# The scan of a diffusion-backbone layer: the turned inverse by whole-array transpositions instead of products of its own

## What is computed

```python
def rwkv7_scan(inputs, s0):
    def step(s, inp):
        r_t, w_t, k_t, v_t, kk_t, a_t = inp
        sa = jnp.einsum('bhvk,bhk->bhv', s, -kk_t)
        s = (s * w_t[:, :, None, :] + sa[..., None] * (kk_t * a_t)[:, :, None, :]
             + v_t[..., None] * k_t[:, :, None, :])
        return s, jnp.einsum('bhvk,bhk->bhv', s, r_t)
    xs = tuple(jnp.moveaxis(z.astype(jnp.float32), 1, 0) for z in inputs)
    s_last, y = lax.scan(step, s0, xs)
    return jnp.moveaxis(y, 0, 1), s_last
```

## Time and the profile before

| | |
|---|---|
| median of 3 runs | 4198.44 us |
| the three runs | 4198.46, 4190.90, 4198.44 us |
| span of the profiled execution | 4190.6 us |
| granted clock, mean | 0.939 |
| stage of the scan | about 1126 to 2395 us |

### The profile page before, as it was taken

How to read it: one execution, slowest core, us unless ns; L and a number is a source line. 1 busy time by engine, 2 the same in 40 slices (tenths; PEclk the granted TensorE clock), 3 DMA queues, 4 the chain that set the end, 5 groups by cost and what they waited for, 6 DMA issues and landing times. The chain is left out here.

```text
span 4190.6 us, 114323 instructions
## 1 busy us (share of the span) xinstructions
PE 3609.0 (86%) x50045; PEld 3216.5 (77%) x50045; DVE 2427.7 (58%) x4367; ACT 1876.2 (45%) x3279; POOL 1273.3 (30%) x1258
## 2 busy tenths in 40 slices
PE   5699999999777777777777678799399999999997
PEld 2578888888677777777777678777299999999987
DVE  3236676630047666767676765433567676666666
ACT  3246665631145554555454544233244344434454
POOL 1223333321056464556554245300101111010202
PEclk8899999999889999999999889899599999999999
DMA  5235555532333333333332267443366667676786
GB/s 171 68 120 177 188 175 170 170 130 72 112 76 92 84 84 80 86 100 86 84 93 66 63 194 224 138 141 115 102 197 206 206 206 216 194 216 200 230 288 226
DMA packets 565269, 612.66 MB, mean 146 GB/s; under 512 B 66018, under 2 KB 469284, under 8 KB 563748
## 3 DMA queue, kind: packets, MB, share of 16 engines
q1 hardware_dynamic: 515620, 493.82, 38.1%
q0 software_dynamic: 22688, 80.75, 6.5%
q10 hardware_dynamic: 26464, 30.77, 2.4%
HBM read 443.62 MB, written 161.50 MB: 144 GB/s over the span
## 5 line engine op out<-in xcount | busy, mean ns | idle before, releaser
L578 PE MATMUL moe_h<-moe_xt_hi,moe_w_hi 128*128 128x256 f32 x2048 | 582.6, 284 | 7.3 <-DVE moe_w_lo L430 3.4
L430 DVE TENSOR_TENSOR moe_w_lo<-moe_w_lo_whole,moe_w_hi 128x2048 fp32r<-128x2048 f32 x254 | 446.3, 1757 | 242.3 <-ACT moe_w_hi L646 195.5
L578 PE MATMUL moe_h<-moe_xt_lo,moe_w_hi 128*128 128x256 f32 x2048 | 580.3, 283 | 0.0
L578 PE MATMUL moe_h<-moe_xt_hi,moe_w_lo 128*128 128x256 f32 x2048 | 580.2, 283 | 0.0
L1963 PE MATMUL inward_pp<-u_u_hi,inward_w_hi 128*128 128x512 f32 (+1 forms) x1360 | 527.6, 388 | 20.6 <-POOL inward_w_lo L2123 20.6
L1963 PE MATMUL inward_pp<-u_u_lo,inward_w_hi 128*128 128x512 f32 (+1 forms) x1360 | 516.0, 379 | 0.0
L1963 PE MATMUL inward_pp<-u_u_hi,inward_w_lo 128*128 128x512 f32 (+1 forms) x1360 | 515.6, 379 | 0.0
L578 PEld LDWEIGHTS moe_h<-moe_xt_hi,moe_w_hi 128*128 128x128 f32 x2048 | 393.4, 192 | 18.3 <-issue 5.8
L578 PEld LDWEIGHTS moe_h<-moe_xt_lo,moe_w_hi 128*128 128x128 f32 x2048 | 393.5, 192 | 3.6
L578 PEld LDWEIGHTS moe_h<-moe_xt_hi,moe_w_lo 128*128 128x128 f32 x2048 | 393.4, 192 | 0.0
L486 POOL DMA_INDIRECT scratch_x<-moe_ys,moe_who x30 | 86.1, 2869 | 863.7 <-DVE moe_ys L752 746.7
(11 more groups left out here) (397 smaller groups left out, 9893.0 us busy)
## 6 DMA issues: line engine op xcount, KB each, us to landing
moe_w_lo_whole<-in_moe_w SPq DMA_DIRECT2D x384, 512.0 KB, 5.1
scratch_ops<-inward_ops SPq DMA_DIRECT2D x72, 514.0 KB, 3.8
scan_over<-scratch_ops SPq DMA_DIRECT2D x72, 512.0 KB, 10.1
inward_w_lo_whole<-in_w_in SPq DMA_DIRECT2D x38, 512.0 KB, 4.5
scan_aq<-scratch_ops SPq DMA_DIRECT2D x36, 516.0 KB, 5.3
scratch_gates<-inward_out SPq DMA_DIRECT2D x64, 256.0 KB, 2.1
all_late<-in_w_mod POOLq DMA_DIRECT2D x32, 512.0 KB, 4.4
rest_modsum<-scratch_gates SPq DMA_DIRECT2D x64, 256.0 KB, 3.4
```

Of the source, the lines that this page charges most:

```text
L430: return nc.vector.tensor_tensor(x_lo, x, x_hi.bitcast(F32), ALU.subtract)
L578: mm = nc.tensor.matmul(hb[ft % 2][m][:, 0:CAP], w_, x_, start=(k == 0 and part == 0), stop=(k == KD - 1 and part == 2))
```

## The change

T and Lt are gone: no product Lt, no mask and no unit addition for T, no T product and no T add in the levels. Instead, at each level `forward` lets PE turn the whole W (four transpositions of 128x128 per unit) behind the F products, into the same pair of PSUM banks, and ACT copies F and the turned W together, 1024 columns, into the new tile FT. A transposition of 128x128 turns two neighbouring blocks and both heads at once, which puts odd and even blocks on different halves of the partitions. F is therefore written by the parity of the block, and F's 16 products and W's 16 products each go over all four quadrants in turn. DVE adds the new part of W through a view of the tile with the parities apart. V moves to r=0 beside L, tK to r=3 beside tB, where V was; r=4 has no product of the solve any more. The waits for the over tiles move from the joint products to r=0.

```diff
@@ -2294,7 +2294,8 @@
         V, La, Lb, Lk = (twice(x) for x in ("V", "La", "Lb", "Lk"))
         over = each("over", [P, 2, 4 * G])
         ob = each("ob", [P, 2, G])
-        W, T, F, L = (each(x, [P, 2, G]) for x in "WTFL")
+        W, L = (each(x, [P, 2, G]) for x in "WL")
+        FT = each("FT", [P, 2, 2 * G])
         aq = each("aq", [P, 2, 2, 2 * G + 4])
...
@@ -2302,7 +2303,8 @@
         Sd = each("Sd", [P, 2, HD])
         X, Z = (each(x, [P, 2, HD]) for x in "XZ")
         y = each("y", [P, 8, HD])
-        bank = [[n.ps(f"b{u}{b}", [P, 512]) for b in range(4)] for u in U]
+        pair = [n.ps(f"pair{u}", [P, 2, 512]) for u in U]
+        bank = [[n.ps(f"b{u}{b}", [P, 512]) for b in range(2)] + [pair[u][:, x, :] for x in range(2)] for u in U]
         masks = n.sb("masks", [P, len(MASKS) * P])
         late, stack = env["late"], env["stack"]
         wm = late[:, 0:NJ * G].rearrange("p (k c) -> p k c", k=NJ)
...
-        level_pe = [x for m in LEVELS for x in (f"F{m}", f"W{m}", f"T{m}")][:-1]
+        level_pe = [x for m in LEVELS for x in (f"F{m}", f"T{m - 1}", f"W{m}")]
         chunks = lambda names: [f"{x}{c}" for c in range(4) for x in names]
 
         def steps(name, names):
@@ -2331,11 +2333,10 @@
         second_done = [EVICTED[FIRST_OF[u][1]][1] + "1" for u in U]
 
-        PE = [Steps(n.sem(f"pe_solve{u}"), ["L", "Lt"] + list(FIRST_OF[u]) + ["tB", "V", "tK"] + level_pe) for u in U]
-        AC = steps("act_solve", ["L", "tB", "V", "tK"] + [f"F{m}" for m in LEVELS])
-        DV = [Steps(n.sem(f"dve_solve{u}"), ["T0"] + [f"{x}{d}" for p in FIRST_OF[u] for x in EVICTED[p] for d in U] +
-                    [f"{x}{m}" for m in LEVELS for x in "TW" if m < 5 or x == "W"]) for u in U]
-        PO = steps("pool_solve", ["T0", "W0"] + [f"H{m}" for m in LEVELS])
+        PE = [Steps(n.sem(f"pe_solve{u}"), ["L", "V"] + list(FIRST_OF[u]) + ["tB", "tK"] + level_pe) for u in U]
+        AC = steps("act_solve", ["L", "V", "tB", "tK"] + [f"F{m}" for m in LEVELS])
+        DV = [Steps(n.sem(f"dve_solve{u}"), [f"{x}{d}" for p in FIRST_OF[u] for x in EVICTED[p] for d in U] + [f"W{m}" for m in LEVELS]) for u in U]
+        PO = steps("pool_solve", ["W0"] + [f"H{m}" for m in LEVELS])
@@ -2361,15 +2362,15 @@
         def four(x):
             return x.rearrange("p d (c f) -> p d c f", f=HD)
 
-        def banked(x):
-            return x[:, :].rearrange("p (d c f) -> p d c f", d=2, f=HD)
+        def halves_of(x):
+            return x[:, :, :].rearrange("p d (q j f) -> p j (d q) f", j=2, f=HD)
+
+        def products(u, half):
+            return pair[u][:, :, half * G:(half + 1) * G]
 
         def masked(name):
             k = MASKS.index(name)
             return masks[:, k * P:(k + 1) * P].rearrange("p (d f) -> p d f", d=2).unsqueeze(2).broadcast_to([P, 2, 4, HD])
-
-        def level_banks(m):
-            return (3, 2) if m % 2 else (2, 3)
 
         def lru_of(k):
             j, q = k // (2 * NG), k % (2 * NG)
@@ -2473,12 +2474,9 @@
                 uB, uK = (0, 1) if r == 1 else (1, 0)
                 for u in U:
                     if r == 1:
-                        AC[u].wait(pe, "L", it)
-                        DV[u].wait(pe, "T0", it)
+                        AC[u].wait(pe, "V", it)
                     else:
                         DV[u].wait(pe, EVICTED[FIRST_OF[u][0]][1] + "1", it)
-                pe.wait_ge(s_over0[uK], 16 * it + 16)
-                pe.wait_ge(s_over1[uK], 16 * it + 16)
                 for k in range(8):
                     mmB = side_by_side(uB, k, of_ops(ob[uB], None, 0), aq[uB][:, b], 0, False)
                     mmK = side_by_side(uK, k, of_ops(over[uK], None, G), over[uK], 2 * G, True)
@@ -2492,16 +2490,13 @@
                 if r == 0:
                     pe.wait_ge(s_aq[u][b], half * 16 + 16)
                     pe.wait_ge(s_ob[u], 16 * it + 16)
+                    pe.wait_ge(s_over0[u], 16 * it + 16)
+                    pe.wait_ge(s_over1[u], 16 * it + 16)
                     DV[u].wait(pe, "W5", it - 1)
-                    two(u, ("L", 2, oA, oB), ("Lt", 3, oA, oB))
+                    two(u, ("L", 2, oA, oB), ("V", 3, xV, unit))
                 elif r == 3:
                     DV[u].wait(pe, second_done[u], it)
-                    two(u, ("tB", 2, oB, unit), ("V", 3, xV, unit))
-                else:
-                    AC[u].wait(pe, "tB", it)
-                    for k in range(8):
-                        mm = one(u, 2, xK, unit, True, k)
-                    PE[u].did("tK", mm)
+                    two(u, ("tB", 2, oB, unit), ("tK", 3, xK, unit))
 
             def forward(u, m, a):
                 it = a[0]
@@ -2510,26 +2505,30 @@
                     DV[u].wait(pe, f"W{m - 1}", it)
                 else:
                     PO[u].wait(pe, "W0", it)
-                    AC[u].wait(pe, "V", it)
-                for k in range(8):
-                    mm = one(u, level_banks(m)[0], of(H[u][(m - 1) % 3]), of(W[u]), True, k)
+                    AC[u].wait(pe, "tK", it)
+                held, old = of(H[u][(m - 1) % 3]), of(W[u])
+                for pos in range(4):
+                    for j in range(2):
+                        k = 2 * pos + j
+                        for x, h in enumerate(HALVES):
+                            mm = nc.tensor.matmul(pair[u][HALVES[j], x, pos * HD:(pos + 1) * HD], held(h, k), old(h, k), start=True, stop=True)
                 PE[u].did(f"F{m}", mm)
+                whole = W[u][:, :, :].rearrange("p d c -> p (d c)")
+                for pos in range(4):
+                    at = G + pos % 2 * P
+                    mm = nc.tensor.transpose(pair[u][:, pos // 2, at:at + P], whole[:, pos * P:(pos + 1) * P], env["ident"])
+                PE[u].did(f"T{m - 1}", mm)
 
             def square(u, m, a):
                 it = a[0]
                 AC[u].wait(pe, f"F{m}", it)
-                if m > 1:
-                    DV[u].wait(pe, f"T{m - 1}", it)
-                else:
-                    PO[u].wait(pe, "T0", it)
-                same, other = level_banks(m)
-                for k in range(8):
-                    w = one(u, other, of(T[u]), of(F[u]), True, k)
-                    if m < 5:
-                        v = one(u, same, of(F[u]), of(T[u]), False, k)
-                PE[u].did(f"W{m}", w)
-                if m < 5:
-                    PE[u].did(f"T{m}", v)
+                mixed = lambda part, pos, x: FT[u][part, x, pos * HD:(pos + 1) * HD]
+                turned = lambda part, pos, x: FT[u][part, pos // 2, G + (2 * (pos % 2) + x) * HD:G + (2 * (pos % 2) + x + 1) * HD]
+                for pos in range(4):
+                    for x, h in enumerate(HALVES):
+                        for j, part in enumerate(HALVES):
+                            mm = nc.tensor.matmul(pair[u][h, j, G + pos * HD:G + (pos + 1) * HD], turned(part, pos, x), mixed(part, pos, x), start=True, stop=True)
+                PE[u].did(f"W{m}", mm)
 
             def state(u, c, step, a):
                 it, b, _ = a
@@ -2607,19 +2606,18 @@
                 if r == 0:
                     PE[u].wait(act, "L", it)
                     PO[u].wait(act, "H5", it - 1)
-                    AC[u].did("L", act.activation(flat(L[u][:, :, :]), bank[u][2][:, :], ACT.Copy))
+                    AC[u].did("L", act.activation(flat(L[u][:, :, :]), bank[u][2], ACT.Copy))
+                    PE[u].wait(act, "V", it)
+                    AC[u].did("V", act.activation(flat(V[u][b][:, :, :]), bank[u][3], ACT.Copy))
                 elif r == 3:
                     PE[u].wait(act, "tB", it)
-                    AC[u].did("tB", act.activation(flat(tB[u][b][:, :, :]), bank[u][2][:, :], ACT.Copy, scale=-1.0))
-                    PE[u].wait(act, "V", it)
-                    AC[u].did("V", act.activation(flat(V[u][b][:, :, :]), bank[u][3][:, :], ACT.Copy))
-                elif r == 4:
+                    AC[u].did("tB", act.activation(flat(tB[u][b][:, :, :]), bank[u][2], ACT.Copy, scale=-1.0))
                     PE[u].wait(act, "tK", it)
-                    AC[u].did("tK", act.activation(flat(tK[u][b][:, :, :]), bank[u][2][:, :], ACT.Copy))
+                    AC[u].did("tK", act.activation(flat(tK[u][b][:, :, :]), bank[u][3], ACT.Copy))
 
             def forward(u, m, a):
-                PE[u].wait(act, f"F{m}", a[0])
-                AC[u].did(f"F{m}", act.activation(flat(F[u][:, :, :]), bank[u][level_banks(m)[0]][:, :], ACT.Copy))
+                PE[u].wait(act, f"T{m - 1}", a[0])
+                AC[u].did(f"F{m}", act.activation(FT[u][:, :, :], pair[u][:, :, :], ACT.Copy))
 
             def state(u, c, step, a):
                 it = a[0]
@@ -2774,36 +2772,25 @@
             def begin(u, r, a):
                 it, b, half = a
                 D = DV[u]
-                if r == 0:
-                    PE[u].wait(dve, "Lt", it)
-                    D.did("T0", dve.tensor_tensor(four(T[u][:, :, :]), banked(bank[u][3]), masked("lev0t"), ALU.mult))
```

(25 more changed lines are left out.)

2 lines of the change are left out of this document (1 added, 1 removed).

## The result

The change takes the layer from 4195.5 us (median of 4 runs on the same chip, 4190.9 to 4198.5) to **4071.4 us** (4 runs, 4067.6 to 4080.6): ratio 0.971, 95% interval 0.970 to 0.972. That is 124 us less; 4113 was forecast. The profiled execution of the change has a span of 4078.8 us at a mean granted clock of 0.939, the same clock as before. Spans fell by 111.8 us, medians by 124: the profiled execution was the slowest of its four.

The account below looks back on a forecast made before the run. It took the scan's 69 us pass, with PE's 4.8 us stop for instructions behind the reload, as where the change lies. Terms -3.6 - 0.4 + 0.7 - 1.2 - 0.3 = -4.8 us, times 17 = -82, gave 4113 us; range 4055 to 4215.

Parts of the forecast that it names:

- the shift: Reload waits for tK, which ends earlier, so the load burst starts about 3.6 us earlier: -3.6 us per pass.
- the slower rival: In the scan, the transpositions let the granted clock fall well under 0.91; 4262 us, chance 0.17.
- T products cost PE nothing beside W products: In the levels, F uses two quadrants, W with T all four; removing T alone gives PE no time.
- Long stop and W1: PE's 4.8 us stop during the reload, and level 1's W: -3.6 us per pass, -0.4 for the clock.
- Levels 2 to 4: ACT's copy of F grows to 1024 columns, +0.47 us each; net +0.7 us per pass.
- Level 5 and the second stop: Bare chain without state work, -1.2 us per pass; short stop at W5/F5, -0.3 for 15% fewer instructions.
- The start: From L to level 1's F: DVE's and POOL's dropped work at the start of a pass gives 0.
- tK's 2.1 us: tK's products leave their own step and run beside tB; costed at nothing, becoming more waiting for Z.
- the wait for Z: PE's wait for DVE's copy of Z behind F1 was to grow to 4 us instead of 2.
- The shift brings nothing: Instruction blocks collide with the reload just as long; only -1.8 us per pass, about 4164 us; chance 0.22.
- The stop goes altogether: PE's long stop vanishes, -7 in place of -3.6 and -0.4, so -7.8 us per pass, 4058 us; chance 0.05.
- ACT's copies take all back: Ten longer ACT copies per pass put 4.7 us on the path: no change, 4191 us; chance 0.06.

Follow-up runs that it names:

- E11: Kernel before, with 14 of 16 T products left out per unit and level, DVE's adds kept (inverse wrong): 4116.4 us, ratio 0.983.
- E4: Changed kernel with F's and W's loops turned round, so successive products use two quadrants at a time: 4080.5 us, ratio 0.973.
- E6: Changed kernel with W turned by sixteen 64x64 products with the unit matrix in place of four transpositions: 4184.5 us, ratio 0.998.
- E10: E6's kernel with E2's light reload (wrong data): 4089.2 us, ratio 0.976.
- E9: Changed kernel with one more DVE addition into a spare tile ahead of W's in levels 1 to 4: 4105.6 us, ratio 0.979.
- E1: Changed kernel with SP's reload waiting for F1 of both units instead of tK, about 4.5 us later: 4095.1 us, ratio 0.975.
- E2: Changed kernel with the reload cut to 8 columns after pass 0, all passes on the first pass's operands (wrong data): 4011.8 us.
- E3: Kernel before with the reload cut to 8 columns after pass 0, all passes on the first pass's operands (wrong data): 4097.8 us.
- E12: Changed kernel with the reload's six loads issued one at a time, behind unit 1's tK, F1, W1, F2, W2 and F3: 4039.1 us, ratio 0.964.
- E7: Changed kernel with the reload in two, unit 0's three loads behind tK, unit 1's behind F2: 4074.0 us, ratio 0.970.
- E5: Changed kernel with each level's four transpositions of W issued twice (same result): 4090.3 us, ratio 0.976.

## Why the prediction was right, and where its steps failed

**Right:** faster, 4071 in the range of 4055 to 4215. The range is wide, and part of this is luck: the gain is 124 us where the sum had 82, and the shift that made up most of the sum, 3.6 us of 4.8, gave an estimated 1.0. The burst comes 3.1 us earlier (3.6 forecast). F's products are 15.4 ns apart (16), the transpositions 0.11 us each, F with transpositions 1.21 to 1.27 us per unit (1.3). The clock did not fall: 0.939 before and after, and 0.92 in both from 1190 to 2130 us, with 720 transpositions that stand in fours between products, so the slower rival did not occur. No run shows the 3 us per level from which its 4262 was added up. ACT's longer copies (1017 ns, 1059 forecast) cost little, in 26 waits of 10.0 us together:

```profile
L2620 ACT ACTIVATE scan_FT<-scan_pair 128x1024 f32<-128x1024 f32 x180 | 178.4, 1017 | 53.0 <-PE scan_pair L2519 51.3 <-issue 1.4
```

**The step that failed** is "T products cost PE nothing beside W products. Removing T alone gives PE no time; halving comes from the new order". It was read from the pace of the products, and each half of it has its run. (The pace itself was read a little high: 34 ns a record is a busy time that includes the last record's own 0.22 us; from start to start F's records before are 30 ns apart, so F had less to gain than forecast.) Removing T alone gives 72 us, at least 46 of them not from the pace (E11). The new order, as far as E4 undoes it, gives 9 us. Giving back the number of instructions at an undiminished pace takes 113 of the 124 away (E6), and costs 77 us without the reload's burst (E10). What a T product cost was not its place in the array but its four instructions, two records of products and two weight loads. The prediction had counted these (280 records per pass, 15%) and then used them only for 0.3 us at the second stop.

**By stretch.** The same distances as in the table above, as differences to the change in us per pass; E11 as a difference to before:

| stretch | before | E6 (instructions back) | E9 (adds back) | E11 less before |
|---|---|---|---|---|
| L to S1 | -0.6 | -0.1 | -0.1 | +1.9 |
| S1 to F2 | +2.9 | +1.0 | -0.3 | -3.7 |
| F2 to W4 | +1.1 | +2.0 | +1.2 | +0.7 |
| W4 to the next L | +2.8 | +2.7 | +0.6 | -2.4 |

**The terms of the sum.** *Long stop and W1, -4.0 with the clock:* -2.9. The stop shrank by 2.3 us. The forecast counted the burst's shift at its full length, 3.6 us for 3.6; in E1 a shift of 4.5 us is worth 1.4, which makes the change's 3.1 us of shift about 1.0 (an estimate in proportion). E2 against E3 puts 38 us, 2.2 per pass, to everything that hangs on the burst. The 0.4 for the clock no run shows by itself. In the 7 us behind the windows of the long stop, sixteen in each kernel, the mean granted clock is 0.69 before (0.50 from 1717.6 to 1720.6 us, behind the stop shown there) and 0.78 in the change; from 1190 to 2130 us it is 0.92 in both. *Levels 2 to 4, +0.7:* -1.1. ACT's copies are there as forecast; they are outweighed by the T adds that no longer stand before W's (given back, in E9, they cost 1.2 us here) and by fewer instructions (given back, in E6: 2.0; in E11 this stretch grows by 0.7 all the same, since stops also move from one stretch to another). The forecast had costed the T adds in level 5 alone. *Level 5 and the second stop, -1.5:* -2.8. With the number of instructions given back, in E6, 2.7 of it are lost, and leaving most T products out of before gives 2.4 (E11); the adds account for 0.6 (E9). The forecast had 0.3 for the instructions here. *The start, 0:* +0.6, most of it in the stretch from L to X0, 4.36 instead of 3.33 us, where some of the 21 stops of L2454 without a releaser now fall. tK's 2.1 us did vanish as forecast, X1 to F1 took 0.8 less and F1 to W1 1.4 more, but the wait for Z did not grow to 4 us; it stayed at 1.9.

The costs of the single parts do not add up (113 for the number, 34 for the adds, 9 for the pace, against a gain of 124): each takes up room in which PE would else wait for another.

**The rivals.** *The shift brings nothing* (4164): it brings little by itself (E1); the two parts that were put too low elsewhere hid that. *The stop goes altogether* (4058): the time came near this rival's, but by another way; the stop is half as long and E12 shows 25 to 32 us still in it. *ACT's copies take all back:* no; 10.0 us of waits. What stays open is the exact split of 86 us between the number of instructions and DVE's adds, since E6 and E10 keep the adds away and E9 the number: 77 + 34 is more than 86.

## What to carry to other kernels

Where an engine works through many small instructions, count the instructions of a pass beside their time: in this kernel a product that ran in the shadow of another in the array still cost its share of the instruction supply (without 224 records per pass and their weight loads 72 us less, at least 46 of them not from the pace; E11), and four whole-array transpositions in place of sixteen products paid, 113 us, although they take as long (F with them 1.27 us per unit, with the products 1.17; E6). A stop without a releaser inside a group of like instructions, ending behind a packet of the instruction queue (here 1.1 to 1.7 us behind it), is the sign. Then look at what fills the DMA engines at that time, and issue large loads one by one over the pass rather than together: two lumps in place of one gave nothing (E7), six single loads gave 25 to 32 us (E12).

## What the runs showed of the hardware

The instruction supply has a pace of its own. In the records of queue 8, over the whole span of all thirteen kernels, two blocks of 16 KB never start less than 3.2 us apart; in the scan before the change the distance is under 3.7 us in a quarter of the cases and 4.0 in the middle. At 252 instructions a block and four to a product, 3.3 us per block are 26 ns per record, while four quadrants take 15.4 and two 24.4 (E4) to 30 (before). My reading is that PE can run at four quadrants' pace only from what it already holds, and that a slower order loses little by it; how much it holds, no run shows. An estimate from these numbers: 1888 records and their weight loads are 15 blocks, at 3.3 us some 49 us of a pass of 69; 1608 are 12.8 blocks, 42 of 63. When a burst holds the DMA engines (two blocks in 11 us), little slack is left to catch up.

The granted clock differs between these kernels, from 1190 to 2130 us: 0.89 in E6, which has the longest stops (up to 7.5 us), 0.92 in the change, and 0.95 in E4 and E5, in which PE has more to do and waits less. So PE work that was added in E4 cost less than its own time. What exactly sets the clock there, no run shows.

The waits at the ends of blocks are there in all of these kernels: fetch gaps are 6.3 us per pass in the change, 8.8 before, 10.4 in E6, and 7.0 in E10, which has only the light reload.
